# Even layer's compression halves made in one slot, forget halves sooner, products of ones in more waits, fewer squares added on GpSimd in three norms

## The chip, the cores and the metric

One core of a Trainium2 chip runs one program. The time is the device time of one execution in microseconds: three runs of the kernel before took 2322.48, 2320.4 and 2325.7 us, median 2322.48.

## The reference

The program computes four transformer sublayer groups in a row on x of 512 tokens by 1024 features, in float32. The first block is a mixer of two attentions (one with an indexer that picks 256 keys, one with latent keys and values), a cross attention to 256 memory tokens and a mixture of 16 experts. The second block has two layers, each with a norm before and after every part:

```python
for layer in range(DEPTH_2):
    h = rms_norm_2(x, g[0])
    y = even_mixer(h, ...) if layer % 2 == 0 else diff_mixer(h, ...)
    x = x + rms_norm_2(y, g[1])
    y = memory_cross_attention_2(rms_norm_2(x, g[2]), mem_n, ...)
    x = x + rms_norm_2(y, g[3])
    y = swiglu(rms_norm_2(x, g[4]), ...)
    x = x + rms_norm_2(y, g[5])
```

The even mixer is what most of the change is about. It has a forget attention (`o_fox`) and a second one with three branches over the same queries (`o_nsa`): keys and values compressed by a small network, selected blocks (here all of them), and a window. The compression is

```python
flat = blocks.reshape(B, nc, G, CMP_BLOCK * dh)     # 31 blocks of 32 tokens
return jax.nn.gelu(flat @ w1) @ w2                  # for keys and for values
o = jnp.concatenate([o_fox, o_nsa], axis=-1);  return o @ w_out
```

## The kernel before

**Layout and products.** Activations lie turned: features on 128 partitions, 512 tokens along them, in 8 tiles. A weight product is split in three to keep float32 accuracy: each operand has a rounded high half and a low half, and high x high, high x low and low x high add up in one PSUM bank. `linear` (L506) makes one output tile in this way; it takes a bank, and then waits for each source tile as it comes to it. A tile of eight 128x128 weight blocks arrives by SyncE's queue; ScalarE makes its high half (L457), and VectorE (even tiles) or GpSimd (odd tiles) its low half (L462). Three tiles of halves are held at once, and a half is free when TensorE has used the tile before.

**Order.** Each engine has its own program (`pe_program`, `act_program`, ...), written out by hand and first run dry to number the semaphores. Every `me.wait_ge(key)` waits for the step that did `me.done(key)`. Banks and buffers come from queues: `take` waits until the last user of the buffer at the head is done. `me.beside` holds a second stream of steps, one of which is put in at each `tick`, so the compression (`compressed_side`, L3453) runs in slots between the steps of the branch attention.

**Products of ones.** `keep_warm` (L500) issues as many 128x128 products of a matrix of ones as `K.warm` has for a key, into a bank whose contents are overwritten afterwards. The kernel before calls it at the start of a group of products and before the spread of a root; `K.warm` (L4072) has eight entries with 92 products.

**Norms.** ScalarE squares each of 8 tiles into one of four `ta` buffers (`squares_act`, L636). GpSimd adds tiles 1 to `LAST_ADDED[st]` to tile 0 (`squares_pool`, L649, the addition is L656). TensorE sums the remaining tiles and the added one over the partitions with ones (`column_sums`, L580), in the order of `summed_tiles`. With 6, two tiles are summed; with 5, three; with 3, five, of which the first three are summed ahead of the last chunk of the group of products (`early_squares_pe`, L671). Then ScalarE takes a root, VectorE inverts it (L737) and TensorE spreads it (L596). `n0` is the norm of the first mixer, where VectorE also computes an angle table (L1489 to L1513) before it comes to the inverse; `n5` and `n8` are those before the two feed-forward parts.

**Ends of attentions.** An attention runs over pairs of heads. In a step TensorE makes the scores of one pair (`products_pe`), turns the probabilities of the pair before (`turn_pe`, L1195), multiplies by the values (L1217) and spreads the sums (L1227). `score_banks` (L1106) takes the banks of a causal pair; a pair of the memory attention is not causal and takes its banks in `products_pe`. After the even mixer's branch attention `even_out` (L3670) makes high and low halves of the forget output ("of") and of the branch output ("on"), both only after the attention's end on TensorE and on VectorE, and `sandwich_pe` (L2279) multiplies them with the output weights: each of its 8 outputs runs over "of" 0 to 3, then "on" 0 to 3. `x1`, `x2`, `x4`, `x5`, `x8` name the output products of the first mixer, the first memory part, the even mixer and the two later memory parts. In the differential attention `diff_products_pe` (L3752) makes scores and `diff_features_pe` (L3876) turns the normed output back.

Of the kernel before, what the change touches and what calls it, by code (L numbers as in the profile page):

```python
# [16 lines left out]
T = 512  # L17
# [7 lines left out]
NCMP = 31  # L25
# [479 lines left out]

def linear(K, me, key, name, layer, columns, src, m=128, n=T, row0=0, after=None, pool="ps", amid=None):  # L506
    bank = K.banks[me.take(pool, *key)]
    for k, (hi, lo, ready) in enumerate(src):
        b = block(K, me, lo is not None, (name, layer, row0 + 128 * k, columns))
        tile, c = b // 8, slice(b % 8 * 128, b % 8 * 128 + m)  # L510
        last, end = k == len(src) - 1, padded(K, b) and not K.plan.dry
        for r in ready:
            me.wait_ge(*r)
        if lo is None:
            me.wait_ge("raw", tile)
            mm = me.e.matmul(bank[0:m, 0:n], raw_of(K, tile)[:, c], hi, start=k == 0, stop=last)
        else:
            me.wait_ge("wh", tile)
            me.wait_ge("wl", tile)
            wh, wl = halves_of_tile(K, tile)  # L520
            me.e.matmul(bank[0:m, 0:n], wh[:, c], hi, start=k == 0, stop=False)  # L521
            me.e.matmul(bank[0:m, 0:n], wh[:, c], lo, start=False, stop=False)  # L522
            mm = me.e.matmul(bank[0:m, 0:n], wl[:, c], hi, start=False, stop=last)  # L523
        if end:
            mm.then_inc(*me.done("wused", tile))
        if amid and k == AMID:
            norm_spread_pe(K, me, amid)
        if last:
            K.plan.tile[key] = tile
            if end:  # L530
                me.alias(*key)
            else:
                mm.then_inc(*me.done("mm", *key))
                me.alias(*key)
    if after is not None:
        me.give(pool, key, *after)
    return bank
# [61 lines left out]
def spread_root(K, me, key, s, inv, after, rows=128, ncol=T, nh=1):  # L599
# [4 lines left out]
    for i in range(ncol // 128):  # L604
# [3 lines left out]
        for g in range(nh):  # L608
# [6 lines left out]

LAST_ADDED = {"n0": 6, "n1": 6, "n2": 6, "n3": 6, "n5": 6, "n6": 6, "n8": 6, ("y", "x4"): 6, ("y", "x7"): 6,
              ("y", ("ffn", 0)): 6, ("y", ("ffn", 1)): 6, ("y", "x5"): 5, ("y", "x8"): 5, "n4": 3, "n7": 3}


def summed_tiles(st):

    if LAST_ADDED[st] == 3:
        return [0, 4, 5, 6, 7]
    if LAST_ADDED[st] == 5:
        return [6, 7, 0]
    return [7, 0] if st in ("n3", "n5", "n6", "n8") else [0, 7]


def tile_sum(st, k):
# [474 lines left out]
def score_banks(K, me, it, key):  # L1106
    for g in range(len(groups(it))):
        for h in range(2):
            if it["causal"] and g == 1 and h:
                K.plan.slot[("S", *key, 1, 1)] = K.plan.slot[("S", *key, 0, 1)]  # L1110
            else:
                me.take("ps", "S", *key, h, g)


def score_ready(it, h, g):
# [70 lines left out]
def turn_pe(K, me, a, p, it):  # L1186
    for h in range(2):
        for pk, pack in enumerate(packs(it)):
            bank = K.banks[me.take("ps", "T", a, p, h, pk)]
            for i in range(NQ):  # L1190
                me.wait_ge("exp", a, p, h, i)
            for j, i0, c0 in pack:
                for i in range(i0, NQ):
                    c = c0 + 128 * (i - i0)
                    tp = me.e.transpose(bank[:, c:c + 128], probs(K, a, p, h, i)[:, 128 * j:128 * j + 128], K.ident)  # L1195
            tp.then_inc(*me.done("T", a, p, h, pk))
            if it["causal"] or (h, pk) != (0, 0):
                me.give("ps", ("T", a, p, h, pk), ("PT", a, p, h, pk))
            if not it["causal"] and (h, pk) == (1, 0):
                me.give_next("ps", ("T", a, p, 0, 0), ("PT", a, p, 0, 0))  # L1200
    me.alias("turned", a, p)
# [127 lines left out]
def pairs_of(items):  # L1329
    return [items[n:n + 2] for n in range(0, len(items), 2)]  # L1330
# [27 lines left out]
    me.alias("end", "pe", a)  # L1358


def attention_act(K, me, a, items, first=(), pt_first=(), ticks=0):
    pairs = pairs_of(items)
    for step in range(len(pairs) + 2):
        p = step - 1
        if step > 1:
            scales_act(K, me, a, p - 1, pairs[p - 1][0])
        me.tick(ticks)
        if 0 <= p < len(pairs):
            for h in range(2):
                turned_copy(K, me, a, p, pairs[p][0], h, pt_free(a, p, pt_first))  # L1370
        for b in range(2):
            if step < len(pairs):
                exp_act(K, me, a, step, pairs[step][0], b, first)
        me.tick(ticks)
    me.alias("end", "act", a)


def attention_dve(K, me, a, items, first=(), pt_first=(), ticks=0, values=None):
    pairs = pairs_of(items)
    for step in range(len(pairs) + 2):  # L1380
        p = step - 1
        if step < len(pairs):
            me.take("sd", "sd", a, step)
        if 0 <= p < len(pairs) and not K.second[a]:
            for h in range(2):
                turned_copy(K, me, a, p, pairs[p][0], h, pt_free(a, p, pt_first))
            sums_dve(K, me, a, p, pairs[p])
        if step < len(pairs):
            max_dve(K, me, a, step, pairs[step][0], 0, first)
        if step > 1:  # L1390
            out_dve(K, me, a, p - 1, pairs[p - 1][0])
        if step < len(pairs):
            max_dve(K, me, a, step, pairs[step][0], 1, first)
        if values and step == 0:
            for n in range(2):
                values_out_dve(K, me, ("mv", values), K.mem_values(values), n, 2)
            ahead(K, me, ("L", ("mq", values), 1))
        me.tick(ticks)
        if 0 <= p < len(pairs) and K.second[a]:
            for h in range(2):  # L1400
                turned_copy(K, me, a, p, pairs[p][0], h, pt_free(a, p, pt_first))
            sums_dve(K, me, a, p, pairs[p])
        me.tick(ticks)
    me.alias("end", "dve", a)
# [2048 lines left out]
def compressed_side(K, me):  # L3453

    e, a = me.e, K.area
# [54 lines left out]
    for s in range(2):  # L3510
        hs = a[0:2 * NCMP, 18, 256 * s:256 * s + 128]
        u = a[0:2 * NCMP, 18, 256 * s + 128:256 * s + 256]
        ht = K.mis[:, 96 + 64 * s:96 + 64 * s + 62]
        if me.name == "dve":
            me.wait_ge("cmp", "tanh", s)
            e.tensor_scalar(u, u, 0.5, 0.5, ALU.mult, ALU.add).then_inc(*me.done())
            me.wait_ge()
            e.tensor_tensor(hs, hs, u, ALU.mult).then_inc(*me.done("cmp", "hact", s))
            me.wait_ge("hidt", s)
            e.tensor_copy(ht, K.bank("hidt", s)[:, 0:2 * NCMP]).then_inc(*me.done("cmp", "hb", s))  # L3520
        if me.name == "pe":
            bank = K.banks[me.take("ps", "hidt", s)]
            me.wait_ge("cmp", "hact", s)
            e.transpose(bank[:, 0:2 * NCMP], hs, K.ident[0:2 * NCMP, 0:2 * NCMP]).then_inc(*me.done("hidt", s))
            me.give("ps", ("hidt", s), ("cmp", "hb", s))
        yield
# [126 lines left out]
def even_act(K, me):  # L3653
# [6 lines left out]
    heads_act(K, me, "nsa", K.i_nsa, "n3", 0)  # L3660
    values_act(K, me, "vsw", K.i_vsw)
    me.beside = compressed_side(K, me)
    attention_act(K, me, "nsa", K.i_branch, [("end", "pe", "fox")], [("pv", "fox", 3)], ticks=2)
    me.flush()
    me.alias("end", "act", "nsa")
    even_out(K, me)
    sandwich_act(K, me, "x4", "n4", "mem1")


def even_out(K, me):  # L3670
    war = [("end", "pe", "nsa"), ("end", "dve", "nsa")]
    parts_of(K, me, "of", 4, 0, lambda c: K.area[:, 20 + c, :], [("whole", "of", c) for c in range(4)], war)
    parts_of(K, me, "on", 4, 8, lambda c: K.O[:, c, :], [("cmp", "add", c) for c in range(4)], war)


def even_dve(K, me):
# [8 lines left out]
    values_dve(K, me, "vsw", K.i_vsw, norm="n3")  # L3685
    me.beside = compressed_side(K, me)
    K.o_last = [("out", "nsa", c) for c in range(4)]
    attention_dve(K, me, "nsa", K.i_branch, [("end", "pe", "fox")], [("pv", "fox", 3)], ticks=2)
    me.flush()
    me.alias("end", "dve", "nsa")  # L3690
    even_out(K, me)
# [4 lines left out]
def even_pool(K, me):  # L3696
# [24 lines left out]
    attention_pool(K, me, "nsa", K.i_branch, ticks=2)  # L3721
    me.flush()
    me.alias("end", "pool", "nsa")
    even_out(K, me)
    mem_load(K, me, "mem1")
    sandwich_pool(K, me, "x4", ("x", "x3"), "n4", "mem1")
# [148 lines left out]

def diff_features_pe(K, me, m):  # L3876
    bank = K.banks[me.take("turns", "feat", m)]
    me.wait_ge("scaled", m)
    for i in range(NQ):
        tp = me.e.transpose(bank[:, 128 * i:128 * i + 128], K.tan("diffn", "dsq", m)[:, 128 * i:128 * i + 128], K.ident)  # L3880
    tp.then_inc(*me.done("feat", m))
    me.give("turns", ("feat", m), ("gained", m))
# [177 lines left out]
def tables(K):  # L4060
# [9 lines left out]
    K.next_norm = {("ffn", 0): "n6", ("ffn", 1): None}  # L4070
    K.before = {("ffn", 0): ("x", "x5"), ("ffn", 1): ("x", "x8")}
    K.warm = {("group", ("mq", "mem1")): 14, ("group", ("mq", "mem2")): 14, ("group", ("ffn", 0)): 12, ("group", ("ffn", 1)): 12,  # L4072
              ("group", "dqk"): 12, ("rot", "mlar"): 16, ("bc", ("lat", 0)): 6, ("bc", "n1"): 6}
    K.o_last = [None] * 4
    order = ["n0", "n1", "n2", "n3", ("y", "x4"), "n4", ("y", "x5"), "n5", ("y", ("ffn", 0)), "n6", ("y", "x7"), "n7",
             ("y", "x8"), "n8", ("y", ("ffn", 1))]
# [214 lines left out]
```

## Time and profile before

| | us |
|---|---|
| median of three runs | 2322.48 |
| the profiled execution | 2324.66 |
| its span | 2322.9 |
| TensorE busy | 2191.3 |
| VectorE busy | 1247.6 |
| ScalarE busy | 1115.7 |
| GpSimd busy | 767.8 |

The span runs from the first to the last instruction of one profiled execution; the profiled execution's own time is 1.8 us more. TensorE's mean granted clock is 0.975 of full speed: it is 1.00 (2.4 GHz) for most of the span and 0.50 (1.2 GHz) in a number of short stretches. A busy time counts overlapping records once, so the share of TensorE says nothing on how fast its products follow each other.

### The profile page before, as it was taken

What the parts mean: (1) busy time and instruction counts of PE and PEld (TensorE: products, weight loads), DVE (VectorE), ACT (ScalarE), POOL (GpSimd) and SP (SyncE); (2) the same over time, 40 slices, a digit from 0 to 9 for tenths busy, and PEclk for the clock granted to TensorE, in tenths of its full rate; (3) what the DMA queues carried; (4) which work ended last, traced back from release to release, by engine and by line L of the source; (5) the groups of instructions that cost most, each with busy time, mean ns of one, the idle gap of its engine ahead of it and who ended that gap; (6) DMA issues with size and microseconds to landing.
All of it is one profiled execution on the core that took longest, in us unless ns stands there. A gap on an engine that the chain in (4) does not pass through costs nothing.

```text
span 2322.9 us, 29928 instructions
## 1 busy us (share of the span) xinstructions
PE 2191.3 (94%) x10776; PEld 1772.2 (76%) x10776; DVE 1247.6 (54%) x2220; ACT 1115.7 (48%) x1956; POOL 767.8 (33%) x501
## 2 busy tenths in 40 slices
PE   7899999889999999988989999999999899999997
PEld 6676777768888787766867888887877777888886
DVE  6777575558999734455456323225567455322223
ACT  5455554457888635554354322224766344332222
POOL 5361233421000322510335332225842435333233
PEclk9999999998999999998999999999999999999998
DMA  4312223217999620230221323322311221323321
GB/s 167 141 37 69 73 92 113 82 73 284 389 394 385 241 91 19 73 100 1 73 73 64 109 91 101 99 95 69 100 64 37 73 73 55 105 95 100 98 94 54
DMA packets 74530, 264.10 MB, mean 114 GB/s; under 512 B 8272, under 2 KB 8400, under 8 KB 74000
## 3 DMA queue, kind: packets, MB, share of 16 engines
q1 hardware_dynamic: 66816, 238.76, 29.7%
q10 hardware_dynamic: 4752, 11.61, 1.4%
q0 software_dynamic: 2816, 11.82, 1.4%
q8 instruction: 87, 1.43, 0.3%
q14 instruction: 59, 0.48, 0.1%
HBM read 247.98 MB, written 14.18 MB: 113 GB/s over the span
## 4 chain that ended last, share of the span: by engine, by line
PE 78%; DVE 7%; ACT 5%; issue 4%; POOL 4%; DMA 2%; POOLq 0%; DVEq 0%; ACTq 0%; SPq 0%
PE ps L521 17%; PE ps L523 17%; PE ps L522 17%; PE ps L1180 3%; PE ps L2938 2%; PE ps L2940 2%; PE ps L2939 2%; PE ps L1195 2%; POOL ta L656 2%; PE ps L1217 2%; PE ps L585 1%; ACT Sb L1304 1%; POOL xT L2398 1%; PE ps L2965 1%; PE ps L2966 1%
## 5 line engine op out<-in xcount | busy, mean ns | idle before, releaser
L457 ACT ACTIVATE wh<-raw 128x1024 fp32r<-128x1024 f32 x308 | 322.6, 1054 | 451.4 <-PE ps L523 413.6
L462 DVE TENSOR_TENSOR wl<-raw,wh 128x1024 fp32r<-128x1024 f32 x176 | 236.4, 1350 | 494.9 <-ACT wh L457 488.9
L521 PE MATMUL ps<-hh,wh 128*128 128x512 f32 (+1 forms) x1192 | 468.5, 393 | 4.8 <-POOL wl L462 4.4
L462 POOL TENSOR_TENSOR wl<-raw,wh 128x1024 fp32r<-128x1024 f32 x132 | 321.7, 2437 | 449.7 <-ACT wh L457 449.6
L523 PE MATMUL ps<-hh,wl 128*128 128x512 f32 (+1 forms) x1192 | 465.5, 391 | 0.0
L522 PE MATMUL ps<-hl,wh 128*128 128x512 f32 (+1 forms) x1192 | 465.2, 390 | 0.0
L521 PE MATMUL ps<-act,wh 128*128 128x512 f32 (+1 forms) x688 | 269.0, 391 | 13.7 <-ACT act L1462 9.9
L522 PE MATMUL ps<-act,wh 128*128 128x512 f32 (+1 forms) x688 | 267.7, 389 | 0.0
L523 PE MATMUL ps<-act,wl 128*128 128x512 f32 (+1 forms) x688 | 267.5, 389 | 0.0
L521 PEld LDWEIGHTS ps<-hh,wh 128*128 128x128 f32 (+1 forms) x1192 | 224.1, 188 | 54.2 <-issue 7.7
L523 PEld LDWEIGHTS ps<-hh,wl 128*128 128x128 f32 (+1 forms) x1192 | 223.9, 188 | 47.8 <-issue 0.4
L522 PEld LDWEIGHTS ps<-hl,wh 128*128 128x128 f32 (+1 forms) x1192 | 224.1, 188 | 46.2 <-issue 0.6
L521 PEld LDWEIGHTS ps<-act,wh 128*128 128x128 f32 x688 | 131.4, 191 | 42.8 <-ACT act L1462 11.6
L656 POOL TENSOR_TENSOR ta<-ta 128x512 f32<-128x512 f32 x82 | 126.8, 1546 | 88.1 <-ACT ta L640 82.7
L523 PEld LDWEIGHTS ps<-act,wl 128*128 128x128 f32 x688 | 131.3, 191 | 26.6
L522 PEld LDWEIGHTS ps<-act,wh 128*128 128x128 f32 x688 | 131.3, 191 | 25.9
L756 POOL TENSOR_TENSOR act<-ta,act 128x512 fp32r<-128x512 f32 x44 | 57.0, 1296 | 277.5 <-ACT act L751 277.5
L713 DVE SCALAR_TENSOR_TENSOR hl<-xT,small,hh 128x512 fp32r<-128x512 f32 x72 | 80.7, 1130 | 18.9 <-ACT hh L705 18.9
L705 ACT ACTIVATE hh<-xT,small 128x512 fp32r<-128x512 f32 x72 | 51.8, 720 | 80.4 <-DVE xT L2398 35.0
L1235 POOL COPY td<-stat 128x512 f32<-128x512 f32 x26 | 15.9, 611 | 218.5 <-DVE stat L1318 132.5
L787 ACT ACTIVATE ta<-td 32x512 f32<-32x512 f32 x132 | 83.1, 630 | 10.2 <-DVE td L973 5.6
L3186 POOL DMA_INDIRECT rows<-d_ys,mis x4 | 7.6, 1906 | 234.0 <-DMA d_ys<-rows 233.0
(471 smaller groups left out, 3960.1 us busy)
## 6 DMA issues: line engine op xcount, KB each, us to landing
raw<-d_w SPq DMA_DIRECT2D x277, 512.0 KB, 3.7
raw_x<-d_moe SPq DMA_DIRECT2D x84, 512.0 KB, 6.6
raw<-d_moe SPq DMA_DIRECT2D x84, 512.0 KB, 6.7
d_xs<-Sb POOLq DMA_DIRECT2D x7, 514.0 KB, 7.7
Xb<-d_xs ACTq DMA_DIRECT2D x6, 514.0 KB, 6.3
area<-d_mem POOLq DMA_DIRECT2D x3, 1024.0 KB, 5.2
d_ys<-rows ACTq DMA_DIRECT2D x6, 512.0 KB, 6.6
xT<-d_x SPq DMA_DIRECT2D x8, 256.0 KB, 6.6
```

The lines of the kernel that those rows point to most:

```text
L457: me.e.activation(hi, raw, ACT.Copy).then_inc(*me.done("wh", m))
L462: me.e.tensor_tensor(lo, raw, hi.bitcast(F32), ALU.subtract).then_inc(*me.done("wl", m))
L521: me.e.matmul(bank[0:m, 0:n], wh[:, c], hi, start=k == 0, stop=False)
L522: me.e.matmul(bank[0:m, 0:n], wh[:, c], lo, start=False, stop=False)
L523: mm = me.e.matmul(bank[0:m, 0:n], wl[:, c], hi, start=False, stop=last)
L656: me.e.tensor_tensor(s, s, K.tan("sq", st, k), ALU.add).then_inc(*me.done("sqa", st, k))
L705: me.e.activation(K.hh[:, k, :], x, ACT.Copy, scale=gain).then_inc(*me.done("hi", st, k))
L713: me.e.scalar_tensor_tensor(K.hl[:, k, :], K.xT[:, k, :], K.gain(st, k), K.hh[:, k, :].bitcast(F32), ALU.mult, ALU.subtract).then_inc(*me. ...
L756: me.e.tensor_tensor(lo, src, hi.bitcast(F32), ALU.subtract).then_inc(*me.done("lo", *key))
L787: me.e.activation(K.ta[r:r + 32, i, :], K.tdn("xh", st, n)[at:at + 32, :], ACT.Copy).then_inc(*me.done("swap", st, n))
L1180: mm = me.e.matmul(K.bank("S", a, p, h, g)[:, c], l, r, start=m == 0, stop=m == len(mats) - 1)
L1195: tp = me.e.transpose(bank[:, c:c + 128], probs(K, a, p, h, i)[:, 128 * j:128 * j + 128], K.ident)
```

## The change

It does five things. (1) `LAST_ADDED` becomes 3 for n0 and 5 for n5 and n8. (2) In the compression, VectorE makes the activations of both halves in the slot of the first. (3) The "of" halves are made before the branch attention's last output instead of after its end, and the "on" halves no longer wait for VectorE's end. (4) `keep_warm` is also called in `linear`, `score_banks`, `turn_pe`, before the transposition of the compression and in `diff_features_pe`. (5) `K.warm` gets entries for these calls.

```diff
@@ linear
     bank = K.banks[me.take(pool, *key)]
+    keep_warm(K, me, key, bank)
@@
-LAST_ADDED = {"n0": 6, "n1": 6, "n2": 6, "n3": 6, "n5": 6, "n6": 6, "n8": 6, ...
+LAST_ADDED = {"n0": 3, "n1": 6, "n2": 6, "n3": 6, "n5": 5, "n6": 6, "n8": 5, ...
@@ summed_tiles
-    return [7, 0] if st in ("n3", "n5", "n6", "n8") else [0, 7]
+    return [7, 0] if st in ("n3", "n6") else [0, 7]
@@ score_banks
                 me.take("ps", "S", *key, h, g)
+                if (h, g) == (0, 0):
+                    keep_warm(K, me, ("S", *key), K.bank("S", *key, 0, 0))
@@ turn_pe
             bank = K.banks[me.take("ps", "T", a, p, h, pk)]
+            keep_warm(K, me, ("T", a, p, h, pk), bank)
@@ attention_act (and the like in attention_dve, ahead of out_dve)
+        if finish and step == len(pairs) + 1:
+            finish(K, me)
         if step > 1:
             scales_act(K, me, a, p - 1, pairs[p - 1][0])
@@ compressed_side
         if me.name == "dve":
-            me.wait_ge("cmp", "tanh", s)
-            e.tensor_scalar(u, u, 0.5, 0.5, ALU.mult, ALU.add).then_inc(*me.done())
-            me.wait_ge()
-            e.tensor_tensor(hs, hs, u, ALU.mult).then_inc(*me.done("cmp", "hact", s))
+            for r in range(2) if s == 0 else ():
+                hr = a[0:2 * NCMP, 18, 256 * r:256 * r + 128]
+                v = a[0:2 * NCMP, 18, 256 * r + 128:256 * r + 256]
+                me.wait_ge("cmp", "tanh", r)
+                e.tensor_scalar(v, v, 0.5, 0.5, ALU.mult, ALU.add).then_inc(*me.done())
+                me.wait_ge()
+                e.tensor_tensor(hr, hr, v, ALU.mult).then_inc(*me.done("cmp", "hact", r))
             me.wait_ge("hidt", s)
...
             bank = K.banks[me.take("ps", "hidt", s)]
+            keep_warm(K, me, ("hidt", s), bank)
             me.wait_ge("cmp", "hact", s)
@@ even_act, even_dve: finish=even_forget_out; even_pool: even_forget_out after its attention
+def even_forget_out(K, me):
+    last = len(pairs_of(K.i_branch)) - 1
+    parts_of(K, me, "of", 4, 0, lambda c: K.area[:, 20 + c, :], [("whole", "of", c) for c in range(4)],
+             [("S", "nsa", last, 1, 1)])
+
 def even_out(K, me):
-    war = [("end", "pe", "nsa"), ("end", "dve", "nsa")]
-    parts_of(K, me, "of", 4, 0, lambda c: K.area[:, 20 + c, :], [("whole", "of", c) for c in range(4)], war)
+    war = [("end", "pe", "nsa")]
     parts_of(K, me, "on", 4, 8, lambda c: K.O[:, c, :], [("cmp", "add", c) for c in range(4)], war)
@@ diff_features_pe
     bank = K.banks[me.take("turns", "feat", m)]
+    keep_warm(K, me, ("feat", m), bank)
@@ tables
-              ("group", "dqk"): 12, ("rot", "mlar"): 16, ("bc", ("lat", 0)): 6, ("bc", "n1"): 6}
+              ("group", "dqk"): 12, ("rot", "mlar"): 16, ("bc", ("lat", 0)): 6, ("bc", "n1"): 6,
+              ("res", "x1", 0): 7, ("res", "x2", 0): 8, ("sw", "x5", 0): 8, ("sw", "x8", 0): 8, ("sw", "x4", 0): 14,
+              ("hidt", 1): 12, ("S", "diff", 1): 8, ("feat", 7): 14}
+    for m in ("mem0", "mem1", "mem2"):
+        K.warm["S", ("matt", m), 1], K.warm["T", ("matt", m), 0, 1, 1] = 8, 5
```

## Rows read from the trace of the kernel before

**Rows 1.** The page: busy share of the engines, and the two weight-half groups.
```profile
PE 2191.3 (94%) x10776; PEld 1772.2 (76%) x10776; DVE 1247.6 (54%) x2220; ACT 1115.7 (48%) x1956; POOL 767.8 (33%) x501
...
L457 ACT ACTIVATE wh<-raw 128x1024 fp32r<-128x1024 f32 x308 | 322.6, 1054 | 451.4 <-PE ps L523 413.6
...
L462 POOL TENSOR_TENSOR wl<-raw,wh 128x1024 fp32r<-128x1024 f32 x132 | 321.7, 2437 | 449.7 <-ACT wh L457 449.6
```

**Rows 2.** Timeline of TensorE: start, time, operation, records; products of ones and of x4.
```profile
455.18 2.60 PE L503 MATMUL ps<-const 128*128 128x128 f32 x12
...
1109.61 0.39 PE L521 MATMUL ps<-act,wh 128*128 128x512 f32 x1
...
1112.12 0.39 PE L523 MATMUL ps<-act,wl 128*128 128x512 f32 x1
...
1227.40 2.84 PE L503 MATMUL ps<-const 128*128 128x128 f32 x24
1230.00 0.47 PE L561 MATMUL ps<-hh,wh 128*128 128x512 f32 x1
```

**Rows 3.** Windows: stretch, its length, busy time (records) per engine, PEclk, DMA, GB/s.
```profile
37.60:40.90 3.30, 3.30 (x9) 2.52 (x9) 1.72 (x3) 0.00 (x0) 3.19 (x2) 0.50 0.56 166
495.00:503.00 8.00, 5.31 (x25) 3.21 (x22) 4.11 (x8) 2.82 (x7) 1.90 (x2) 1.00 0.61 208
1034.30:1041.00 6.70, 5.84 (x25) 4.81 (x27) 2.50 (x12) 2.70 (x7) 0.44 (x1) 0.50 0.00 0
1102.50:1109.10 6.60, 4.44 (x11) 3.43 (x12) 5.42 (x5) 4.27 (x8) 4.67 (x4) 0.50 0.00 0
1211.70:1215.00 3.30, 3.30 (x9) 2.52 (x8) 0.69 (x1) 2.02 (x3) 1.92 (x1) 0.50 0.11 20
```

**Rows 4.** Timeline of TensorE; in brackets the idle time before, and its releaser.
```profile
36.65 0.65 PE L596 MATMUL ps<-const,rt 128*128 128x128 f32 x4 [4.42 <-DVE rt L737]
...
499.12 0.47 PE L521 MATMUL ps<-act,wh 128*128 128x512 f32 x1 [2.08 <-ACT act L1462]
...
1035.16 0.34 PE L3524 MATMUL ps<-const,area 62*128 62x62 f32 x1 [3.85 <-DVE area L3518]
...
1104.66 0.76 PE L521 MATMUL ps<-act,wh 128*128 128x512 f32 x1 [3.64 <-ACT act L1462]
...
1209.88 0.47 PE L521 MATMUL ps<-act,wh 128*128 128x512 f32 x1 [2.08 <-ACT act L1462]
...
1255.88 0.47 PE L521 MATMUL ps<-hh,wh 128*128 128x512 f32 x1 [1.42 <-POOL wl L462]
...
1706.32 2.43 PE L3761 MATMUL ps<-area 64*128 64x128 f32 x16
...
1815.16 0.66 PE L3880 MATMUL ps<-const,ta 128*128 128x128 f32 x4 [3.37 <-DVE ta L3982]
```

**Rows 5.** Timeline of all engines in the first norm, and the later cast.
```profile
15.90 7.39 POOL L656 TENSOR_TENSOR ta<-ta 128x512 f32<-128x512 f32 x4
...
23.77 2.63 DVE L1489 CAST PT<-O 128x512 f32<-128x512 int32 x1
...
28.20 1.95 PE L585 MATMUL ps<-const,ta 128*128 128x128 f32 x16
...
29.90 0.47 PE L521 MATMUL ps<-hh,wh 128*128 128x512 f32 x1
...
89.46 0.41 DVE L1489 CAST PT<-O 128x512 f32<-128x512 int32 x1
```

**Rows 6.** Timeline of TensorE and GpSimd at the end of norm n5.
```profile
1252.51 1.95 PE L585 MATMUL ps<-const,ta 128*128 128x128 f32 x16
...
1248.02 4.43 POOL L656 TENSOR_TENSOR ta<-ta 128x512 f32<-128x512 f32 x3
```

**Rows 7.** Timeline of TensorE: turns of the branch attention after two pairs.
```profile
1035.42 4.53 PE L1195 MATMUL ps<-const,S_h 128*128 128x128 f32 x20
...
1092.09 2.77 PE L1195 MATMUL ps<-const,S_h 128*128 128x128 f32 x20
```

More of the change, by code:

```diff
@@ L612, in spread_root @@
     me.give("ps", key, *after)
-LAST_ADDED = {"n0": 6, "n1": 6, "n2": 6, "n3": 6, "n5": 6, "n6": 6, "n8": 6, ("y", "x4"): 6, ("y", "x7"): 6,
+LAST_ADDED = {"n0": 3, "n1": 6, "n2": 6, "n3": 6, "n5": 5, "n6": 6, "n8": 5, ("y", "x4"): 6, ("y", "x7"): 6,
               ("y", ("ffn", 0)): 6, ("y", ("ffn", 1)): 6, ("y", "x5"): 5, ("y", "x8"): 5, "n4": 3, "n7": 3}
@@ L1358, in attention_pe, with attention_act @@
     me.alias("end", "pe", a)
-def attention_act(K, me, a, items, first=(), pt_first=(), ticks=0):
+def attention_act(K, me, a, items, first=(), pt_first=(), ticks=0, finish=None):
     pairs = pairs_of(items)
@@ L1375, in attention_act, with attention_dve @@
     me.alias("end", "act", a)
-def attention_dve(K, me, a, items, first=(), pt_first=(), ticks=0, values=None):
+def attention_dve(K, me, a, items, first=(), pt_first=(), ticks=0, values=None, finish=None):
     pairs = pairs_of(items)
@@ L1389, in attention_dve @@
             max_dve(K, me, a, step, pairs[step][0], 0, first)
+        if finish and step == len(pairs) + 1:
+            finish(K, me)
         if step > 1:
@@ L3662, in even_act @@
     me.beside = compressed_side(K, me)
-    attention_act(K, me, "nsa", K.i_branch, [("end", "pe", "fox")], [("pv", "fox", 3)], ticks=2)
+    attention_act(K, me, "nsa", K.i_branch, [("end", "pe", "fox")], [("pv", "fox", 3)], ticks=2,
+                  finish=even_forget_out)
     me.flush()
@@ L3687, in even_dve @@
     K.o_last = [("out", "nsa", c) for c in range(4)]
-    attention_dve(K, me, "nsa", K.i_branch, [("end", "pe", "fox")], [("pv", "fox", 3)], ticks=2)
+    attention_dve(K, me, "nsa", K.i_branch, [("end", "pe", "fox")], [("pv", "fox", 3)], ticks=2,
+                  finish=even_forget_out)
     me.flush()
@@ L3723, in even_pool @@
     me.alias("end", "pool", "nsa")
+    even_forget_out(K, me)
     even_out(K, me)
```

## The prediction

> **What bounds the kernel now.** I read the page first, then the granted clock of chosen stretches, then TensorE's timeline around each edited line, then the other engines there. TensorE is busy in 94% of the span [rows 1]. A 128x512 product follows the one before it after 0.228 us (the 13th product of the first x4 output starts at 1109.61 us, the 24th at 1112.12) [rows 2], so where TensorE runs without a gap only fewer products or a faster clock help. What is left are its waits, and what follows some of them: with the clock granted at 0.50 (1.2 GHz) products take twice as long. Such stretches of 3.3 to 6.7 us stand behind six of the waits that the change touches (x8 and the features have the one of x5 again, at 1921.7 and 1815.9), and half of each is lost [rows 3]. So an edit is worth the part of a wait that it removes plus half of the low stretch behind it, if that goes too; an edit that puts products in front of work that is ready costs their full time.
>
> **Price of the products of ones.** 12 of them (24 records, two each) take TensorE from 1227.40 to 1230.00, 0.217 us each at 2.4 GHz; six at 455.18 take 2.60 us, 0.43 each at 1.2 GHz [rows 2]. Counting the calls in the diff: the three entries for the second score of the memory attentions are never used, because score_banks is called for causal items alone and these are not causal. Eleven waits get products: 7+8+8+8+14+12+8+14 and three times 5, 94 in all, 20 us if none lay in a wait.
>
> **First norm (n0).** Today two tiles are summed before the root; the 16 records go from 28.20 to 29.90, 0.85 us a tile. Nine products later TensorE waits 4.42 us for the root's inverse, until 36.65 [rows 4, 5], and the clock is 0.50 from 37.6 to 40.9 [rows 3]. New: three tiles more, 2.55 us, partly inside that wait. TensorE would reach the spread at 32.23 + 2.55 = 34.8, if the inverse is there. It is late today because VectorE computes an angle table first, and GpSimd slows it: the cast at 23.77 takes 2.63 us beside GpSimd's low halves, the same cast at 89.46 takes 0.41 [rows 5]. GpSimd drops three of the four additions of 1.85 us (15.90 to 23.29) [rows 5], so VectorE works alone for some us, and its table should be done about 2 to 4 us sooner. A new wait comes in: ScalarE's square of tile 7 now needs the buffer of tile 4, which TensorE frees only just ahead of its last chunk of nine products (28.20 less 9 x 0.23, plus two tiles: 27.8). Queued behind it on ScalarE are two high halves of weights, GpSimd's low half behind the first, then the next product. The square takes some 0.6, a high half 1.05, a low half 2.44 in the mean [rows 1]: 31.9. TensorE wants it at 29.90 + 2.55 = 32.45, so it just fits. Gain 1.8 us of wait and half of the low stretch, 1.65. Bounds: +3.8 (all of it), and -1.5 if the low half is late by the longer GpSimd time and VectorE gains nothing. I take +3.4.
>
> The Trainium skill (SBUF — State Buffer, "Who interferes with whom") says that VectorE and GpSimd share a port pair as an exclusive lock, so the second to start waits for the whole instruction. The cast's 2.63 against 0.41 us agrees. By that rule the moved low half (29.5 to 32) would block the end of VectorE's table, and the sum here would be +1.9 rather than +3.4.
>
> **n5 and n8.** One addition of 1.48 us less on GpSimd (three take 4.43), whose low half behind them starts that much sooner, and one tile more on TensorE, 0.85. The two sums from 1252.51 end at 1254.2 today and the next product starts at 1255.88, with 1.42 us of idle time for that low half [rows 4, 6]. New: 1252.51 + 2.55 = 1255.06. The low half, started at 1248.02 + 2 x 1.48 = 1251.0, is done by about 1253.5 (mean 2.44). +0.8 each; bounds 0 (low half no sooner) less 0.85, and +0.8. n8 has the same pattern. I take +1.5 for both.
>
> **Compression in one slot, 12 products before the second transposition.** That transposition waits 3.85 us for VectorE's activation of the second half and starts at 1035.16; the clock is 0.50 from 1034.3 to 1041.0 [rows 3, 4]. With both activations made in the first slot (two operations of some 0.5 us together, before the first copy), the data is there. TensorE is free at 1031.3 (1035.16 less 3.85), the 12 products take 2.6, the transposition follows at 1033.9: 1.3 us. The 20 transpositions behind it take 4.53 us, the like at full clock 2.77 [rows 7]: 1.7. ScalarE's copies and exponentials follow them and the next scores wait for ScalarE, so I carry the sum on: +2.9. Bounds: 0 (ScalarE is late for its own reasons) and +3.9.
>
> **Forget halves sooner, 14 products.** ScalarE makes the four high halves while it waits for the last spread, VectorE puts two subtractions (some 1.4 us) ahead of its last output, so that output and the last addition come 1.4 us later; nobody but the fourth "on" half waits for that. GpSimd does its two at once. TensorE ends at 1101.0 and waits 3.64 us until 1104.66 [rows 4]. New: 14 x 0.217 = 3.0, first product at 1104.1. The "on" halves no longer wait for VectorE's end; I place the last one on GpSimd at about 1107, TensorE wants it at 1104.1 + 21 x 0.228 = 1108.9. The clock was 0.50 from 1102.5 to 1109.1 [rows 3]; without it the 24th product starts at 1109.3 and not at 1112.12 [rows 2]: +2.8. The load of the memory on GpSimd moves forward with its halves, more than TensorE does. Bounds: -2.6 (the 14 products at 0.43 less the wait) and +2.8.
>
> **8 products before x2, x5, x8; 7 before x1.** Each of the first three waits 2.08 us (499.12; 1209.88; x8 is the same at 1920.25), the products take 1.74 and end inside. Behind x5 and x8 the clock is 0.50 for 3.3 us, behind x2 it stays 1.00 [rows 3, 4]. +1.6 for x5, +1.6 for x8, 0 for x2. At x1 there is a like wait, but at the eighth chunk; 1.5 us put before the first moves into it: 0. Bounds each: -1.4 and +1.65.
>
> **14 before the last features.** That wait is 3.37 us (to 1815.16), the products take 3.0 and a little more for a slow start; then 0.50 from 1815.9 to 1819.2 [rows 3, 4]. +1.6; bounds -0.3 and +1.65.
>
> **8 before the second differential score.** The products at 1706.32 start with no wait before them [rows 4]: 1.75 us in front of ready work. Queued behind are the scores, the turn of the first values, and VectorE, which needs both and is dense from there to the combination that TensorE awaits before its first turn. So that wait is not shortened, it moves. -1.75; bounds -1.75 and 0 (plus 1.65 if the low stretch behind goes).
>
> **5 before a turn, three times.** 1.1 us each ahead of a wait for ScalarE's exponentials, and ScalarE, not TensorE, ends the stage: 0; bounds -1.1 and 0 each.
>
> **Sum.** 3.4 + 1.5 + 2.9 + 2.8 + 3.2 + 1.6 - 1.75 = 13.65 us. The profiled execution took 2324.66 us (span 2322.9, 1.8 around it), giving 2311.0; it lies 2.2 above the median of the three, 2322.48, which gives 2308.8. I say 2310.
>
> **Rivals.** What a measurement here can tell from no change is 0.2%, 4.6 us: faster is under 2317.8, slower over 2327.1.
> (a) Half of the clock's part does not come. Rows: after equal waits of 2.08 us the clock fell once (1209.88) and once not (499.12) [rows 3, 4]; so other waits, moved in time, may fall in, and those filled may not have cost in the median run. Half of 1.65 + 1.7 + 2.3 + 3 x 1.6 = 10.5 is 5.2: 2315.2. The Trainium skill (TensorE: Matmul & The Clock Gate, "What's actually happening") says that the activity window runs freely, not from the kernel's start; the trace agrees with the two waits, and by it a filled wait pays only in a share of the executions. Chance 0.20.
> (b) None of it comes: 2310 + 10.5 = 2320.5, no change. For it: the products of ones are light. Against: behind the 12 at 1227.40 no low stretch stands. Chance 0.09.
> (c) Slower: the products meet a clock that is already low, as those at 455.18 did [rows 2]. Then 94 x (0.43 - 0.217) = 20 us more is put before ready work: 2330. It decides where the clock is 0.50 when a wait begins; here that holds only for the features' wait. Chance 0.03.
> (d) The three unused entries do act: two low stretches in the memory attentions go as well, 3.3 us more: 2306.7. Against: the calls. Chance 0.03.
> My forecast, 2304.5 to 2315, has 0.65. Faster 0.65 + 0.20 + 0.03 and a bit of (a) lost to noise: 0.87; same 0.10; slower 0.03. The range 2303 to 2318 takes in (a), (d) and the unknown cost at n0.
>
> **What would show it.** Right: no wait above 1 us before the n0 spread and no 0.50 behind it; the second compression transposition about 2.6 us after the scores; the first x4 product 3 us after the last compression product at clock 1.00; full clock behind x5, x8 and the features. The score at n=1 starting 1.8 us later against its linear than today shows the loss. Wrong: a wait for GpSimd's low half before the fourth product of n0, or low stretches in other places of the same total.

## The result, and the profile after

The changed kernel takes 2311.08 us in the median of five runs (2308.16 to 2311.61), the kernel before 2320.99 (2317.94 to 2325.7): the ratio on record is 0.9941, with a 95% interval of 0.9921 to 0.9962 (the two medians alone give 0.9957, which lies in it). The profiled execution has a span of 2309.8 us against 2322.9. The page after; the first and third lines answer to [rows 1]:

```profile
PE 2202.7 (95%) x11004; PEld 1785.9 (77%) x11004; DVE 1248.8 (54%) x2220; ACT 1115.8 (48%) x1956; POOL 754.8 (33%) x496
...
L462 POOL TENSOR_TENSOR wl<-raw,wh 128x1024 fp32r<-128x1024 f32 x132 | 319.6, 2422 | 461.9 <-ACT wh L457 461.6
```

TensorE is busy 11 us longer and the span is 13 us shorter, so TensorE idles 24.5 us less. The added products alone would take about 25 us at full clock (an estimate: 94 of 0.217 us and five tiles of squares of 0.85), so its other products took some 13 us less: the gain is in part less waiting and in part a higher clock. GpSimd has five additions fewer. The record counts say how many entries of the list act: the instructions of keep_warm in the kernel after, then in the kernel before (duration least, median, most; first and last start).

```profile
L503 PE MATMUL ps<-const x372: 271/275/582, 102.1 to 1928.0; 128*128 128x128 f32 x186
```
```profile
L503 PE MATMUL ps<-const x184: 271/275/582, 104.5 to 1940.2; 128*128 128x128 f32 x184
```

188 more records are 94 products: the three entries for the memory attentions' scores are never used.

TensorE's timeline at the edited places (bracket: idle time ahead, and its releaser), answering to [rows 4] and [rows 5]:

```profile
32.05 1.95 PE L586 MATMUL ps<-const,ta 128*128 128x128 f32 x16
35.89 0.38 PE L597 MATMUL ps<-const,rt 128*128 128x128 f32 x2
...
1029.13 2.94 PE L503 MATMUL ps<-const 128*128 128x128 f32 x24
1032.01 0.27 PE L3536 MATMUL ps<-const,area 62*128 62x62 f32 x1
...
1094.35 5.01 PE L503 MATMUL ps<-const 128*128 128x128 f32 x28
1099.11 0.48 PE L522 MATMUL ps<-act,wh 128*128 128x512 f32 x1
...
1202.18 0.47 PE L522 MATMUL ps<-act,wh 128*128 128x512 f32 x1 [0.29 <-ACT act L1470]
...
1696.06 1.95 PE L503 MATMUL ps<-const 128*128 128x128 f32 x16
1697.93 2.43 PE L3781 MATMUL ps<-area 64*128 64x128 f32 x16
...
1708.58 0.73 PE L3794 MATMUL ps<-const,Sb 128*128 128x128 f32 x3 [2.18 <-DVE Sb L3996]
...
1806.10 0.66 PE L3901 MATMUL ps<-const,ta 128*128 128x128 f32 x4 [0.66 <-DVE ta L4003]
```

The waits of 4.42, 3.85, 3.64, 2.08 and 3.37 us are gone or down to 0.66 us or less. The one of 2.18 us behind the second differential score is there in full, after 1.9 us of ones put before ready products. And the 14 products before x4 took 4.76 us, not 3.04. Windows of the kernel after (columns as in [rows 3]) say why:

```profile
37.60:40.90 3.30, 3.30 (x17) 2.71 (x16) 1.01 (x2) 1.09 (x2) 2.92 (x2) 1.00 0.16 63
107.90:111.20 3.30, 3.30 (x11) 2.72 (x10) 0.75 (x1) 2.40 (x3) 0.00 (x0) 0.50 0.21 79
522.20:540.00 17.80, 14.39 (x126) 14.22 (x126) 15.27 (x63) 12.14 (x17) 5.08 (x3) 1.00 0.20 58
1034.30:1041.00 6.70, 5.20 (x40) 3.54 (x40) 1.88 (x9) 5.61 (x19) 0.61 (x1) 1.00 0.00 0
1094.40:1097.80 3.40, 3.40 (x18) 3.40 (x17) 3.26 (x6) 1.82 (x4) 1.66 (x1) 0.50 0.01 2
1203.00:1206.30 3.30, 2.69 (x12) 2.17 (x12) 0.69 (x1) 1.61 (x3) 2.93 (x2) 1.00 0.00 0
1806.00:1809.30 3.30, 3.20 (x16) 2.75 (x17) 0.79 (x2) 1.58 (x2) 1.48 (x2) 1.00 0.00 0
```

Full clock behind the first norm, the transposition, x5 and the features, where [rows 3] have 0.50; but 0.50 at 1094.4, over the ones themselves, and at 107.9, where the kernel before has full clock (it has a low stretch of the same length at 71.6 instead). And a stretch that no edit touches, the transpositions of the token rows at 522 us, went from 0.50 to 1.00. This is the kernel before there, in both of its traces:

```profile
522.20:535.80 13.60, 12.73 (x60) 12.57 (x60) 11.30 (x57) 7.95 (x12) 2.53 (x2) 0.50 0.10 37
```
```profile
528.40:542.00 13.60, 12.73 (x60) 12.57 (x60) 11.40 (x57) 8.06 (x12) 2.57 (x2) 0.50 0.10 38
```

The full clock there is worth nothing, though. TensorE then waits longer for VectorE, and for a transfer, behind it; the kernel after, then the kernel before:

```profile
540.78 0.47 PE L2946 MATMUL ps<-wh_x,XT 128*128 128x512 f32 x1 [3.01 <-DVE XT L3137]
555.44 1.09 PE L2931 MATMUL ps<-const,Xb 128*128 128x128 f32 x8 [1.89 <-DMA Xb<-d_xs]
```
```profile
543.42 0.47 PE L2938 MATMUL ps<-wh_x,XT 128*128 128x512 f32 x1 [0.94 <-DVE XT L3129]
```

From the first of these transpositions to the first product that reads Xb it is 35.7 us in the kernel before and 35.4 in the kernel after; over all fourteen traces of this document it is 35.6 to 37.3 us with the low clock and 35.4 to 37.4 with the full one.

All low stretches together are 116.6 us in the kernel before and 80.9 in the kernel after. Which part of that belongs to the edits was left to the experiments.

One more difference is no edit's. The kernel before waits 3.64 us for a transfer in the mixture of experts, with a low stretch behind:

```profile
790.72 1.54 PE L2976 MATMUL ps<-const,rows 128*128 128x128 f32 x10 [3.64 <-DMA rows<-d_ys,mis]
```

The kernel after has neither, and gains 5.8 us on it here. So does the second trace of the kernel before: of the other thirteen traces one has 1.55 us of this wait, and twelve have none.

### The profile page after: what moved, and what is told of

It is laid out like the page before. It is cut to its first block, busy times and chain, and to the rows that moved or that the text cites. A ratio compares the mean times of both kernels' runs of the same rounds, so it can differ in the third digit from the quotient of the medians.

```text
span 2309.8 us, 30375 instructions
## 1 busy us (share of the span) xinstructions
PE 2202.7 (95%) x11004; PEld 1785.9 (77%) x11004; DVE 1248.8 (54%) x2220; ACT 1115.8 (48%) x1956; POOL 754.8 (33%) x496
## 4 chain that ended last, share of the span: by engine, by line
PE 79%; DVE 7%; ACT 6%; issue 4%; POOL 3%; DMA 1%; POOLq 0%; DVEq 0%; ACTq 0%; SPq 0%
PE ps L522 17%; PE ps L524 17%; PE ps L523 17%; PE ps L1183 3%; PE ps L2946 2%; PE ps L2948 2%; PE ps L2947 2%; PE ps L1199 2%; PE ps L586 2%; PE ps L1221 1%; ACT Sb L1308 1%; PE ps L568 1%; PE ps L517 1%; PE ps L562 1%; PE ps L2973 1%
## 5 line engine op out<-in xcount | busy, mean ns | idle before, releaser
L522 PE MATMUL ps<-hh,wh 128*128 128x512 f32 (+1 forms) x1192 | 468.0, 393 | 1.9 <-POOL wl L462 1.6
L522 PE MATMUL ps<-act,wh 128*128 128x512 f32 (+1 forms) x688 | 265.6, 386 | 3.6 <-POOL act L1476 1.8
L523 PE MATMUL ps<-act,wh 128*128 128x512 f32 (+1 forms) x688 | 264.3, 384 | 0.0
L657 POOL TENSOR_TENSOR ta<-ta 128x512 f32<-128x512 f32 x77 | 119.6, 1554 | 80.3 <-ACT ta L641 75.7
L788 ACT ACTIVATE ta<-td 32x512 f32<-32x512 f32 x132 | 83.2, 630 | 10.2 <-DVE td L974 5.6
L562 PE MATMUL ps<-hh,wh 128*128 128x512 f32 (+1 forms) x184 | 75.0, 408 | 10.7 <-DVE wl L462 10.1
```

Of the source, the lines that this page charges most:

```text
L562: me.e.matmul(bank[0:m, :], wh[:, c], hi, start=first, stop=False)
L657: me.e.tensor_tensor(s, s, K.tan("sq", st, k), ALU.add).then_inc(*me.done("sqa", st, k))
L788: me.e.activation(K.ta[r:r + 32, i, :], K.tdn("xh", st, n)[at:at + 32, :], ACT.Copy).then_inc(*me.done("swap", st, n))
```

## Experiments

Each kernel was timed against the kernel before in the same session (medians of before: 2322.99 in 25 runs, 2324.07 in 17, 2322.78 in 23). Single times of one kernel lie 3 to 30 us apart, so terms of 1 to 3 us are read from traces, as differences of the starts of the same instructions, and only groups of terms from times.

**The changed kernel again.**

> The changed kernel once more, unedited, for a second trace. Theory (each filled wait takes away a low stretch for good): 2311 us, full clock again behind the first norm's spread, x5, x8 and the last features, and a clock of 0.50 again at 107.9, 145.4, 452.6, 1046.6 (10 us long), 1094.4, 1186.5 and 1893.1 us. Rival (where the clock falls is in part a draw of the execution): the same 2311 us within 0.15%, but two or more of these stretches gone and others in places where the first trace has none; and the waits without an edit before them at 537.8 us (3.0 us, VectorE) and the one of 3.6 us for the transfer at 787 us of the kernel before come or go with it.

2312.93 us (8 runs), ratio 0.9944 (0.9919 to 0.9969). Between the two: the time is 0.08% off, and of the seven stretches listed one is gone. Behind n0, x5, x8 and the features the clock is full again, and 0.50 again at 107.9, 145.4, 452.6, 1046.5, 1186.5 and 1893.0; the one over the ones before x4 is gone,

```profile
1095.14 3.39 PE L503 MATMUL ps<-const 128*128 128x128 f32 x28
1098.29 0.48 PE L522 MATMUL ps<-act,wh 128*128 128x512 f32 x1
```

so that the 14 products take 3.15 us and the 24th x4 product starts at 1103.60 instead of 1104.44; new ones stand at 258.1, 411.7, 555.0 and 1067.0. The transfer's wait at 787 us is absent here too.

**No products of ones.**

```diff
-              ("res", "x1", 0): 7, ... ("hidt", 1): 12, ("S", "diff", 1): 8, ("feat", 7): 14}
-    for m in ("mem0", "mem1", "mem2"): ...
```

> The changed kernel without any of the thirteen new groups of products of ones; the sums of three norms, the compression in one slot and the forget halves stay. Theory (the products pay by the clock that they keep): a low stretch is back behind x5, x8 and the last features (1.6 us each) and behind the first x4 product (2.2 us), the product before the second differential score is gone (-1.5 us), in all about +5 us: 2316. Rival (the 12 products before the second compression transposition and the 14 before x4 now stand in front of ready work, since the edits beside them have already ended those waits: the data of x4's first product is there at about 1094.9 us and the product starts at 1099.1): 2.6 and up to 3.5 us come back at these two, the first x4 product follows the last compression product after about 0.7 us, and the total is about 2311, no slower than with the products.

2308.72 us (7 runs, 2302.91 to 2319.35), ratio 0.9933 (0.9904 to 0.9962): no slower than with them. The rival holds for the time, the theory for the places where a wait follows: without ones 4.7 us are lost again at x5, x8 and the features, and as much comes back where ones stood before ready work (below: 1.6 us at the second score, 1.7 to 2.0 at the transposition, 1.3 to 2.9 at x4). TensorE of this kernel, first at x4, then at x5, and windows of both:

```profile
1102.39 0.47 PE L522 MATMUL ps<-act,wh 128*128 128x512 f32 x1 [0.58 <-issue]
...
1206.64 0.47 PE L522 MATMUL ps<-act,wh 128*128 128x512 f32 x1 [2.08 <-ACT act L1470]
```
```profile
1207.30:1210.60 3.30, 2.87 (x8) 1.97 (x7) 0.08 (x1) 0.92 (x3) 3.06 (x2) 0.50 0.00 0
1102.40:1109.00 6.60, 5.83 (x23) 4.22 (x24) 5.10 (x6) 1.81 (x4) 3.69 (x3) 1.00 0.12 19
```

Without ones x4 follows the compression after 0.58 us and at full clock: the edit beside them had already ended this wait. x5 has its wait and its low stretch back.

**The products of ones alone.**

```diff
+    keep_warm(K, me, key, bank)      # in linear, score_banks, turn_pe, hidt, features; and the new entries
```

> The kernel before with the thirteen groups of products of ones alone; sums, compression and forget halves as before. Theory: they fill the waits of 3.85, 3.64, 3.37 and twice 2.08 us and the clock stays high behind: gains of 1.7, 2.2, 1.6, 1.6, 1.6, less 1.5 at the second differential score: about 7 us, 2314. Rival (the clock's part is a draw): the waits are filled and TensorE starts each next product at the same time as before, but as many low stretches stand elsewhere: within 2 us of the kernel before, 2319 to 2323.

2319.64 us (12 runs), ratio 0.9976 (0.9960 to 0.9993): 5.6 us by the ratio, 3.4 by the medians, between the theory's 7 and the rival's 2. The terms of its trace, read as in the table below, add to 6.0. Low stretches behind x5, x8 and the features are gone. At x4 the ones (1099.68, 28 records) ran at 0.50 for 3.4 us and took 4.8 us, and the first x4 product came 1.1 us later from the turns ahead than in the kernel before.

**The first norm undone, and alone.**

```diff
-LAST_ADDED = {"n0": 3, ...       # undone: 6, in the changed kernel; alone: 3, in the kernel before
+LAST_ADDED = {"n0": 6, ...
```

> The changed kernel with the first norm's sums as in the kernel before (TensorE sums two tiles of squares, GpSimd adds six). Theory: 3.4 us slower, 2314.5: the wait of 4.4 us before the spread is back with a low stretch behind it, and the lag of 3.0 us at 74 us stays to the end. Rival (the gain is given back before the first attention, as the first trace of the changed kernel shows, whose lead of 3.0 us at 74 us is gone at 144 us: a VectorE operation of 1.59 us for 0.48, and low stretches at 107.9 and 145.4): the same time within 1 us, 2311, with no low stretches at those two places.

> The kernel before with the first norm's sums of the changed kernel alone. Theory (the lead of 3 us that the trace of the changed kernel has at 74 us is kept, and undoing the edit cost 3.3 us): 3 us faster than the kernel before, 2320 to 2321; in the trace the spread's wait of 4.42 us is gone. Rival (it is given back before the first attention): within 1 us of the kernel before.

Undone: 2315.7 us (11 runs), ratio 0.9958 (0.9941 to 0.9975) against 0.9941 and 0.9944 with it. Alone: 2319.44 us (12 runs), ratio 0.9972 (0.9950 to 0.9995). The medians say 3 us twice; alone it is a gain with some certainty (1 to 12 us by the interval), undone the intervals overlap. The theory stands. Of what the rival saw given back by 144 us, one half is a draw: VectorE's operation ahead of the wait there takes 1.59 us in the changed kernel, 0.48 in the kernel before, and 1.59 in its second trace:

```profile
142.28 1.59 DVE L1700 TENSOR_SCALAR td<-area,small 32x512 f32<-32x512 f32 x1
```
```profile
143.14 0.48 DVE L1692 TENSOR_SCALAR td<-area,small 32x512 f32<-32x512 f32 x1
```
```profile
143.15 1.59 DVE L1692 TENSOR_SCALAR td<-area,small 32x512 f32<-32x512 f32 x1
```

The other half, the low stretch at 107.9, comes with the edit in eight of nine traces and costs 1.6 us (see the section on why).

**x4 without its 14; the transposition without its 12; both and the score without its 8.**

```diff
-("sw", "x4", 0): 14                                           # first kernel
-("hidt", 1): 12                                               # second
-("sw", "x4", 0): 14, ("hidt", 1): 12, ("S", "diff", 1): 8     # third
```

> The changed kernel without the 14 products of ones before x4. Theory (they stand in front of ready work, as the trace without any product of ones shows: first x4 product 0.58 us after the last compression product, against 4.8 us with them): the first x4 product 4.1 us sooner, no wait over 1 us in the stage, no low stretch behind; 2307 us. Rival (they keep the clock for x4 and the following linear): the product is sooner by 4.1 us but the 24 products of x4 run at 0.50 (+5.5 us) or wait for the halves of the others: 2311 to 2312.

> The changed kernel without the 12 products of ones before the second compression transposition. Theory (data there since 1024.8, products end 2.9 us later): the transposition 2.6 to 3.0 us sooner, some 1.1 us of it given back because VectorE is still at its maxima when the turned tiles come: 2309. Rival: the whole is given back at the next scores, which wait for ScalarE (1.50 us at 1040.0 in the changed kernel, then longer), 2311; or the clock falls in the wait of the turns: 2312.

> The changed kernel without the three groups of ones that stand in front of ready work: 14 before x4, 12 before the second compression transposition, 8 before the second differential score. Theory (each costs what it takes, and keeps no clock there): -4.1, -1.9 and -1.5 us: 2303.5. Rival (the kernel without any ones showed a lower clock, 0.978 against 0.982 in the median, and these three had a share in it): 2308 to 2311.

First: 2308.0 us (6 runs), ratio 0.9940 (0.9917 to 0.9963). Its x4:

```profile
1095.75 0.47 PE L522 MATMUL ps<-act,wh 128*128 128x512 f32 x1 [0.58 <-issue]
1099.43 0.47 PE L522 MATMUL ps<-act,wh 128*128 128x512 f32 x1 [0.67 <-DVE act L1476]
```

From the turns ahead (the same product at 1078.65 and 1079.40) the first x4 product comes 4.1 us sooner and the 24th 2.9, since later ones now wait for VectorE's half; the window from 1099 to 1106 is at 1.00. Against the second trace of the changed kernel, whose ones met full clock, it is 2.5 and 1.3 us. The theory's mechanism is shown; the ratio alone can't tell it.
Second: 2312.45 us (12 runs), ratio 0.9954 (0.9939 to 0.9969), as if nothing were gained. In the trace it takes 11.73 us from the first transposition to the next scores (1030.70 to 1042.43) against 13.30 (1026.72 to 1040.02), 1.6 sooner; then an additional low stretch of 3.4 us begins at 1042.7 and costs about as much. From the values ahead of the transposition to the next scores it is 12.9 us in all five traces without these ones and 14.6 to 14.9 in the four with them: the ones' price of 1.7 to 2.0 us is shown. That they keep the clock is not: the low stretch at this place stands in three of those five and in one of those four (the kernel with n0 undone).
Third: 2306.42 us (6 runs), ratio 0.9928 (0.9903 to 0.9953), between the two expectations (2303.5, and 2308 to 2311).

**Forget halves sooner alone.** (The kernel before with the edits in attention_act, attention_dve and even_out.)

> The kernel before with the forget halves sooner alone, no product of ones. Theory: the first x4 product stands 0.6 us after the last compression product for 3.64, the later chunks wait for their halves 0.8 us more, and the low stretch behind goes since its wait is gone: 3.1 - 0.8 + 2.2 = 4.5 us, 2319. Rival (the clock stays low, 0.50 through x4's first products): 2.3 us, 2321.

2321.84 us (12 runs), ratio 0.9996 (0.9978 to 1.0014), inconclusive: the interval reaches from 5 us faster to 3 us slower. The trace has x4 at 1096.23 behind 0.58 us of idle time, 3.1 us nearer to the turns of the attention, and its 24th product 3.6 us nearer, with a low stretch of 3.4 us at 1097.0 instead of one of 6.8.

**Ones only where a wait follows at once, run twice.**

```diff
-("res", "x1", 0): 7, ("sw", "x4", 0): 14, ("hidt", 1): 12, ("S", "diff", 1): 8, the three ("T", ...): 5
+            if (i, h) == (0, 0) and a != ("matt", "mem0"):      # in products_pe, behind the take of its bank
+                keep_warm(K, me, ("S", a, p), K.bank("S", a, p, 0, 0))
```

> As the kernel before this one in the list, and also without the 7 ones before x1 and the 5 before three turns, whose two edges cancel in the traces (+1.5 and -1.5 us, +1.1 and -1.2 us), and with 8 ones before the scores of the second pair of the memory attentions of mem1 and mem2, where TensorE waits 2.34 us for VectorE two products later and the clock falls behind it (1186.5 and 1893.1 us). Theory: the low stretches there go, 1.7 us each, 2300 us. Rival: the ones delay the two products that are ready and VectorE's work with them, so the wait moves: 2303 to 2305, the low stretches move behind it.

> The fastest kernel so far once more, unedited (ones only where a wait follows at once): if its 2303.1 was a draw of the clock, 2307 to 2309; if it is the edits, 2301 to 2305. In the trace the stretch of 17 us at 0.50 over the transpositions of the token rows (523.7 to 540.8 us), which five traces so far have and four do not, can be there or not, at 8 us.

2303.08 and 2304.54 us (6 runs each), ratios 0.9914 (0.9890 to 0.9939) and 0.9919 (0.9900 to 0.9938). The mean of the 12 runs is 2303.4, that of the 13 runs of the changed kernel 2311.1; by the ratios this kernel is 5 to 7 us faster than the changed one. That the first time was a draw (2307 to 2309 expected for the second) is out. The wait in the memory attention in the changed kernel, then TensorE at that place in this one, and two windows of it at the place of the old low stretches; behind them those of the changed kernel:

```profile
1185.87 2.34 PE L1183 MATMUL ps<-sel,area 64*128 64x256 f32 x12 [2.34 <-DVE sel L1053]
```
```profile
1180.66 0.70 PE L1185 MATMUL ps<-sel,area 64*128 64x256 f32 x2
1181.51 0.70 PE L1185 MATMUL ps<-sel,area 64*128 64x256 f32 x4 [0.16 <-DVE sel L1053]
```
```profile
1182.90:1186.30 3.40, 3.40 (x24) 2.28 (x21) 3.33 (x12) 3.12 (x11) 0.00 (x0) 1.00 0.47 157
1886.00:1889.40 3.40, 3.40 (x30) 2.86 (x26) 3.37 (x9) 3.12 (x12) 0.00 (x0) 1.00 0.36 118
```
```profile
1186.60:1189.90 3.30, 3.30 (x15) 2.30 (x14) 3.27 (x10) 1.88 (x8) 0.00 (x0) 0.50 0.43 144
1893.20:1896.50 3.30, 3.23 (x14) 2.51 (x14) 3.25 (x9) 2.67 (x10) 0.00 (x0) 0.50 0.20 43
```

The wait of 2.34 us is down to 0.16 and the clock stays full: the theory's mechanism, though the time is in the rival's range (from the third kernel above, at 2306.4, it is the 3.4 us forecast). The clock there is full at both places in both traces of this kernel; in the twelve traces without these ones it is low at 20 of the 24 places, and full at both in the third kernel above. In the first of the two traces the token rows are at 0.50 for 17.1 us, in the second not at all, and the times are the same within 1.5 us.

**The kernel before again.**

> The kernel before, unedited, for a second trace. If low stretches are a draw in part: the one over the token rows' transpositions (13.7 us at 522.2), or those at 153 to 177 us, differ by a stretch or more from the first trace; those behind waits over 2 us (1034, 1102, 1211, 1815, 1921) are there again.

2320.49 us, span 2318.7. Of the five low stretches behind long waits four are there in full and the one at 1034 is 3.4 us long, not 6.8; the token rows have the same 13.7 us, 146 to 180 us has 20.5 us of low clock against 10.2.

## Why the prediction was right

2310 was forecast, 2311.08 measured, by the mechanism named: waits shortened and the clock kept behind them. As totals, the rival of half the clock's part (2315.2) and the one of none (2320.5) are out. Term by term, from starts of the same instructions in the kernel before and in the two traces of the kernel after (us):

| step | forecast | first trace | second trace | how it is read |
|---|---|---|---|---|
| n0 | 3.4 | 3.6 | 3.6 | a product ahead of the norm to one behind the low stretch: 18.96 to 43.08, now 20.14 to 40.66 |
| n5, n8 | 1.5 | 1.6 | 1.6 | a product ahead of the sums to the first behind them: 5.86 to 5.09, and 10.10 to 9.26 |
| one slot, 12 ones | 2.9 | 2.8 | 3.1 | values to next scores: 1027.69 to 1045.37, now 1025.12 to 1040.02 |
| forget halves, 14 ones | 2.8 | 1.1 | 2.7 | turns to the 24th x4 product: 1085.25 to 1112.12, now 1078.65 to 1104.44; 1079.44 to 1103.60 in the second trace |
| x5, x8 | 3.2 | 3.1 | 3.1 | from the attention's turns to behind the low stretch: 13.42 to 11.80, and 16.89 to 15.39 |
| x1, x2, three turns | 0 | 0 | 0 | 1.5 us later before, 1.5 sooner behind x1; 1.1 and 1.2 at a turn |
| features | 1.6 | 1.6 | 1.6 | 8.79 to 7.16 |
| second score | -1.75 | -1.6 | -1.6 | from the linear ahead of it: 16.31 to 17.93 |
| sum | 13.65 | 12.2 | 14.1 | |

Against the second trace of the kernel before, the line of the one slot is 2.0 and 2.3, since that trace is itself 0.8 us faster there; the other lines are the same within 0.3.

The terms are well forecast, the forget halves in the first trace apart; that the whole agrees as closely is in part luck. The profiled spans differ by 13.1 us against the first trace of the kernel before and by 8.9 against its second. In the first pair 5.8 us of it is the transfer's wait at 787 us with its low stretch, which no edit touches. About as much goes the other way: 1.2 us by a later start of the first group of products, 1.6 at 107.9, and 2.7 between 143 and 160 us, by VectorE's operation and the clock.

**n0.** The account was right in substance: VectorE was held up by GpSimd, and its table is done at 30.80 us (last operation) instead of 35.31. The moved half came later than I put it, but in time:

```profile
30.37 0.43 DVE L1521 TENSOR_SCALAR PT<-PT 128x512 f32<-128x512 f32 x1
31.94 2.54 DVE L462 TENSOR_TENSOR wl<-raw,wh 128x1024 fp32r<-128x1024 f32 x1 [1.14 <-ACT wh L457]
...
31.03 2.37 POOL L462 TENSOR_TENSOR wl<-raw,wh 128x1024 fp32r<-128x1024 f32 x1 [13.09 <-ACT wh L457]
```

GpSimd's half starts at 31.03, after the table's end, so the clash that would have made it +1.9 did not meet the table, and 3.6 us were gained. It met VectorE's own half, 2.54 us instead of 1.22 at the same place before, with the root's inverse queued behind it (34.48), still before TensorE asks at 35.9. By the lock that the Trainium skill describes (SBUF — State Buffer, "Who interferes with whom") the second to start is blocked until the first ends: the trace agrees, the half starting at 31.94 ends 1.08 us after GpSimd's at 33.40, and alone it takes 1.22. (In the operations at 144 us the one recorded first is the one that pays, in eleven of fourteen traces; see the last section.) The spread is at 35.9 where I had 34.8, with no wait before it: all products of the first group are 1.2 us later in this trace, and by up to 1.1 us in traces without the edit, so the clash has no part in that.

What the forecast left out comes later. Eight of the nine traces with this edit have a low stretch at 106.6 to 108.1 us, over products that follow each other without a gap, and it costs 1.6 us: the lead over the kernel before (how much sooner the same product starts) is 2.4 us at 101.84 and 0.9 at 114.14. Four of the five traces without the edit have it at 71.0 to 73.0 instead, over the first attention's scores, where it costs nothing: the lead is 2.4 us ahead of it and behind it. So some 2.0 of the 3.6 us are left by 115 us. Why the stretch stands elsewhere was not tried.

**Forget halves.** This is the term that was mis-sized, in the first trace by 1.7 us, in the second by 0.1: "New: 14 x 0.217 = 3.0, first product at 1104.1". The ones met a clock of 0.50 in that trace, as in rival (c), which I had given to the features alone. In the second trace they did not. The larger miss is that I took the 14 as filling a wait: the edit beside them had already ended it, and they stand in front of ready work, at 2.9 us net in the first trace and 1.3 in the second. The halves alone bring the 24th product 3.6 us nearer in the trace of the run without ones, though it meets a low stretch of 3.4 us. The 12 ones of the transposition are the same miss: one slot without them takes 12.9 us from the values to the next scores, for 17.7 before and 14.9 with them.

**Of the clock.** Behind x5, x8 and the features all five traces without ones have the low stretch and all nine with ones have full clock; behind n0's spread all five without that edit have it and none of the nine with it. At these waits it is no draw. The chance of 0.20 on half of the clock's part rested on an equal wait at x2, where only one of the five traces without ones has a low stretch (504.1 in the run without ones). Over the ones before x4 and in stretches that no edit touches it is one; the stretch at 107.9 goes with the n0 edit in eight of nine traces. The free-running window of the Trainium skill (TensorE: Matmul & The Clock Gate, "What's actually happening"), as the prediction read it, would make each place a draw; the traces agree at x4 and at the places without an edit, and not at x5 and x8.

**What stays open.** The share of the forget halves in the time: their interval, 0.9978 to 1.0014, is wider than the term. What the 12 ones do to the clock behind them. Why the token rows fall into either clock was not tried either; it need not be a pure draw, since six of the seven traces with the ones before x1 and the turns have full clock there and six of the seven without them the low one. It costs no time here.

## What to carry to other kernels

Put products of ones only where the wait is still there after the other edits: look at what stands behind them in the new trace, and if the next product starts with no idle time ahead, take them out. Two edits for one wait are not a sum; here leaving out 56 of the 94 and putting 16 ahead of two waits that had none took another 7.7 us off by the means (in the traces 1.3 to 2.9 us at x4, 1.7 to 2.0 at the transposition, 1.6 at the second score and twice 1.6 in the memory attentions). And take two traces of each kernel before a low stretch of the clock, or a wait for a transfer, is put down to an edit. A stretch at full clock is a gain only if nothing behind it waits for another engine: at the token rows it was worth nothing.

## What the runs showed of the hardware

- Over the 128-column products that transpose the token rows the clock was 0.50 for 13.7 to 17.1 us in seven of the fourteen traces, with TensorE busy 12.73 of 13.6 us, and 1.00 all through or nearly so in the other seven. In the seven low ones it stayed low through that busy time, while behind x5, with 3.2 busy of 3.2 us, it was back after one stretch of 3.4 us. The full clock saved 4.0 to 5.6 us up to the first product that reads the turned rows (XT), and longer waits for VectorE and a transfer took them back: 35.4 to 37.4 us up to the first that reads Xb, against 35.6 to 37.3.
- A VectorE operation of 0.48 us that starts 0.05 us before one of GpSimd's takes 1.59 us in eleven traces, and in three it takes 0.48 and GpSimd's takes 1.55 instead of 1.26. The same instruction, the same order of recorded starts: who pays is a draw, and here it sets a wait of TensorE (1.38 or 0.27 us).
